# The S5 recurrence of a hybrid decoder step in chunks of four tokens

## The chip, the cores and the metric

The kernel runs as one program on one core of a Trainium2 chip. The metric is the device time of one execution in microseconds (us); the median of three runs of the kernel before is 1443.91 us (1443.73 to 1446.78).

## The reference, cut to what matters

One step of a single-layer decoder for a prompt of 512 tokens and 8 samples of one token each. Both are normalised, projected by `w_in`, sent through sparse attention (compressed, selected and window branches) and an S5 state-space branch, merged by gates, and sent through an MLP. The part that the change touches is the S5 branch: 32 groups of 16 channels, each with 64 complex states.

```python
def s5(u, h0, w):
    uc = u.reshape(b, t, S5_GROUPS, S5_CH)
    a_bar = exp(lam * dt)
    b_bar = ((a_bar - 1.0) / lam)[..., None] * b_c
    bu = einsum('gnc,btgc->btgn', b_bar, uc)
    h_t = a_bar * h_{t-1} + bu_t            # over the tokens, complex
    y = einsum('gcn,btgn->btgc', c_c, h).real + d * uc
    return y, h[:, -1]
...
z = gelu(y_s5)
o_s5 = z * sigmoid(z @ w['s5_w_glu'] + w['s5_b_glu'])
```

The last state of the prompt and the states of the samples are outputs too.

## The kernel before, in words

Everything is fp32. Activations lie transposed (`hT`: features on partitions, 520 columns: 512 prompt tokens and 8 samples). SyncE (queue SP) brings weights through three slabs of `stream`, in the order of `PLAN`; GpSimd (POOL) gathers the pages of the compression cache into the same slabs. A slab is filled when the slab three places ahead has been used (`slab_used`).

The projection stage, from about 22 to 280 us of the span, is a hand-written order of units for TensorE (PE): `HEAD_UNITS`, then `REST_UNITS`. A unit ("gemm", ...) is 16 matmuls of 128x128 weights on 260 columns (line 1710; each fp32 matmul is two records in the trace); "tr" transposes a K/V tile back to tokens on partitions (line 1687, five transposes). Units use two PSUM pairs in turn, so that unit u waits in `open_pair` until ScalarE (ACT) has evacuated unit u-2 (`pair_free`). ACT works the units off in the same order.

S5 is woven in. The 2048 complex states are 16 blocks of 128 states (2 groups each). The head transposes the padded B table in eight "bb" units, the rest begins with eight "cc" units for C, "h0" (sample states) and "bus" (their inputs, 32 small matmuls, line 1795). VectorE (DVE) builds tables of cos and sin of the state's angle, 512 tokens wide, for the first four blocks (`extend`, lines 1225 to 1230), POOL those of the later twelve. Then `s5_slot` is called 19 times behind the units of `SLOT_AFTER`: it computes B u of one block into PSUM (line 1803, 32 rows of weights, 512 columns) and the outputs of earlier blocks from their states (line 1821). Each block is one pass of the DVE loop (lines 1293 to 1316): rotate the inputs back by the angle, two real scans over 512 tokens, rotate forth. Such a pass waits for `bu_full` and releases `bu_free`, on which the next slot waits on PE; its end is `h_ready`, on which the output matmuls wait. The D term is added by DVE (`y_evac`, line 1256), the gelu is done on ACT after the stage (line 996).

When the stage ends, PE transposes the last states (`st_full`) and begins the compression stage: DVE transposes gathered rows (`permute`, line 1333), PE multiplies them with `w1c` (`layer1`, line 1864). Its first two halves come from the prompt's own rows with 128 columns, the later ones from the gathered slabs with 256. Key scores, selection, attention and the gated branches follow; from 742 us to the end PE works through the large products at line 2108.

## Time and profile before

| | |
|---|---|
| median of three runs | 1443.91 us (1443.73 to 1446.78) |
| span of the profiled execution | 1408.0 us |
| time of the profiled execution itself | not listed with the profile; the median lies 35.9 us above the span |
| PE busy, whole span | 1288.7 us, 92% |
| DVE busy | 935.1 us, 66% |
| ACT busy | 291.7 us, 21% |
| POOL busy | 423.6 us, 30% |
| mean granted TensorE clock | 0.974 |

### The profile page before, as it was taken

How to read it: one execution, taken by the hardware profiler on the slowest of the kernel's cores; microseconds unless marked ns; L12 is line 12 of the kernel's file. 1: busy time of each engine (PE TensorE's matmuls, PEld its weight loads, DVE VectorE, ACT ScalarE, POOL GpSimd, SP SyncE). 2: the span in 40 equal slices, each digit the busy share in tenths (PEclk: the TensorE clock that was granted, in tenths of full speed). 3: DMA queues.
4: the chain of work that ended last, by engine and by line, in shares of the span. 5: the costliest groups of instructions: out<-in, count | busy, mean ns of one | idle time of the engine just before them, and what ended most of it. 6: DMA issues, size and time to landing. Idle time of an engine off the chain costs nothing.

```text
span 1408.0 us, 19662 instructions
## 1 busy us (share of the span) xinstructions
PE 1288.7 (92%) x7155; PEld 1003.8 (71%) x7155; DVE 935.1 (66%) x1469; ACT 291.7 (21%) x849; POOL 423.6 (30%) x455
## 2 busy tenths in 40 slices
PE   5899899899988787889999999996999999999996
PEld 4677567577765554555577888785788888888885
DVE  7999999977763437776775565657565465466445
ACT  3311110010004455554421101014000000000012
POOL 5187290122255702222202111110111112423442
PEclk9999999999998999999999999997999999999998
DMA  8101461176664754433364313332112213122101
GB/s 272 61 16 35 94 133 60 60 264 253 257 215 145 240 180 117 136 117 103 126 240 136 105 60 105 133 123 75 58 62 71 109 60 119 61 73 107 60 1 61
DMA packets 122911, 165.59 MB, mean 118 GB/s; under 512 B 37504, under 2 KB 91312, under 8 KB 118464
## 3 DMA queue, kind: packets, MB, share of 16 engines
q1 hardware_dynamic: 105328, 104.69, 23.7%
q0 software_dynamic: 8080, 50.58, 10.1%
q10 hardware_dynamic: 9408, 9.07, 2.0%
q8 instruction: 57, 0.93, 0.3%
q14 instruction: 38, 0.31, 0.1%
HBM read 158.85 MB, written 13.84 MB: 123 GB/s over the span
## 4 chain that ended last, share of the span: by engine, by line
PE 69%; DVE 18%; issue 5%; ACT 4%; POOL 3%; DMA 1%; SPq 0%; DVEq 0%; PEldq 0%; ACTq 0%
PE PS L2108 42%; PE PS L1864 8%; PE PS L1710 6%; PE PS L1687 4%; POOL stream L801 3%; ACT R L1049 2%; DVE small L1499 2%; PE PS L1961 2%; PE PS L1993 2%; PE PS L2043 1%; DVE QO L1304 1%; DVE PS L1497 1%; DVE QO L1308 1%; DVE QO L1309 1%; DVE QO L1307 1%
## 5 line engine op out<-in xcount | busy, mean ns | idle before, releaser
L1710 PE MATMUL PS<-hT,stream 128*128 128x260 f32 (+1 forms) x800 | 182.2, 387 | 3.0 <-ACT small L957 1.0
L1710 PEld LDWEIGHTS PS<-hT,stream 128*128 128x128 f32 (+1 forms) x800 | 149.1, 189 | 36.3 <-issue 6.6
L2108 PE MATMUL PS<-R,stream 128*128 128x260 f32 x720 | 168.9, 383 | 2.4 <-PE PS L2108 2.4
L2108 PEld LDWEIGHTS PS<-R,stream 128*128 128x128 f32 x720 | 135.7, 190 | 25.8 <-issue 5.5
L2108 PE MATMUL PS<-R 128*128 128x260 f32 x576 | 130.8, 383 | 3.3 <-DVE R L1662 2.1
L1617 DVE TENSOR_TENSOR R<-PS,R 128x260 f32<-128x260 f32 x100 | 42.6, 426 | 126.1 <-PE PS L2108 125.0
L2108 PE MATMUL PS<-R,QO 128*128 128x260 f32 x544 | 123.6, 383 | 1.4 <-DVE QO L1543 1.4
L2108 PEld LDWEIGHTS PS<-R 128*128 128x128 f32 x576 | 109.3, 190 | 21.1 <-DVE R L1662 2.5
L1864 PE MATMUL PS<-R 128*128 128x256 f32 (+1 forms) x544 | 120.1, 377 | 2.7 <-PE PS L1864 2.3
L2108 PEld LDWEIGHTS PS<-R,QO 128*128 128x128 f32 x544 | 103.3, 190 | 17.6 <-DVE QO L1543 1.8
L1864 PEld LDWEIGHTS PS<-R 128*128 128x128 f32 x544 | 98.9, 190 | 20.9 <-issue 8.3
L1617 DVE TENSOR_TENSOR KVU<-PS,KVU 128x260 f32<-128x260 f32 x92 | 39.2, 427 | 101.2 <-PE PS L2108 90.8
L2108 PE MATMUL PS<-hT,stream 128*128 128x260 f32 x384 | 94.8, 390 | 3.7 <-PE PS L2108 3.1
L1687 PEld LDWEIGHTS PS<-consts,R 128*128 128x128 f32 (+2 forms) x465 | 49.6, 140 | 60.0 <-ACT R L1058 42.6
L1687 PE MATMUL PS<-consts,R 128*128 128x128 f32 (+2 forms) x465 | 65.9, 282 | 27.0 <-ACT R L1058 22.8
L580 POOL TENSOR_SCALAR R<-R,small 128x128 f32<-128x128 f32 (+3 forms) x64 | 48.4, 760 | 136.3 <-DVE small L1504 136.3
L2108 PEld LDWEIGHTS PS<-hT,stream 128*128 128x128 f32 x384 | 73.1, 193 | 18.7 <-issue 6.9
L1049 ACT ACTIVATE R<-PS,small 128x128 f32<-128x128 f32 (+3 forms) x128 | 66.1, 525 | 85.6 <-DVE small L1499 66.8
L1102 ACT ACTIVATE R<-PS 128x260 f32<-128x260 f32 x56 | 21.5, 386 | 270.4 <-PE PS L2108 270.4
L794 POOL DMA_INDIRECT stream<-in_cache_kv_cmp,row_cmp x32 | 31.7, 991 | 146.1 <-PEq L1853 82.2
L1333 DVE STREAM_TRANSPOSE R<-stream 128x2048 f32<-128x2048 f32 (+1 forms) x34 | 74.5, 2225 | 0.3
L801 POOL DMA_INDIRECT stream<-in_cache_kv_slc,row_kv x64 | 62.4, 976 | 40.5 <-issue 18.9
(373 smaller groups left out, 2107.9 us busy)
## 6 DMA issues: line engine op xcount, KB each, us to landing
stream<-in_cache_kv_slc SPq DMA_DIRECT2D x192, 128.0 KB, 2.2
stream<-in_w_mlp_up SPq DMA_DIRECT2D x8, 2048.0 KB, 8.7
stream<-in_w_mlp_down SPq DMA_DIRECT2D x8, 2048.0 KB, 8.6
stream<-in_w_in SPq DMA_DIRECT2D x4, 2048.0 KB, 11.7
stream<-in_state_kv_win SPq DMA_DIRECT2D x16, 512.0 KB, 7.5
stream<-in_w_in SPq DMA_DIRECT2D x8, 1024.0 KB, 18.8
out_kv_win_sample<-in_state_kv_win POOLq DMA_DIRECT2D x1, 8176.0 KB, 42.8
stream<-in_w_in SPq DMA_DIRECT2D x16, 256.0 KB, 4.5
```

Of the source, the lines that this page charges most:

```text
L580: return eng.tensor_scalar(S, S, ainv[:, k:k + 1], gtm[:, t, col:col + 1], ALU.mult, ALU.mult)
L794: pool.indirect_dma_start(slab(n)[:, 2048 * c:2048 * c + 2048], None, cmp_rows, bass.IndirectOffsetOnAxis(ap=row_cmp[:, 4 * b + 2 * half + ...
L801: pool.indirect_dma_start(dst[:, x, :], None, slc_rows, bass.IndirectOffsetOnAxis(ap=row_kv[:, at:at + 1], axis=0)).then_inc(rows_in[n % N ...
L1049: ins = nc.scalar.activation(PP[:, n % 2, j, c0:c0 + P * (t + 1)], score_block(n, j, c0), ACT.Exp, bias=amx[:, k:k + 1], accum_out=asm[:, ...
L1333: V.transpose(ROWST[:, w % 3, 0:256 * ns].rearrange("p (s x) -> p s x", x=256), slab(s)[:, 0:512 * ns].rearrange("p (s k x) -> p k s x", k ...
L1499: V.reduce_max(amx[:, k:k + 2 * nx], S[:, :, 0:P * (t + 1)], AX, negate=True).then_inc(as_max, 1)
L1617: V.tensor_tensor(to, product_of(w, i), other, ALU.add).then_inc(pr_added, 1)
L1687: return nc.tensor.transpose(out, in_, ident[0:rows, 0:rows])
L1710: ins = M(pair(u)[0:w, hf, 0:HALF], lhs[k], rhs[k][:, HALF * hf:HALF * hf + HALF], start=(k == 0), stop=(k == n - 1))
L1864: ins = M(out, w1c[:, kind, x, :], rhs, start=(x == 0), stop=(x == 7))
L1961: ins = M(score_block(n, j, c0), qT[64 * j:64 * j + 64, 4 * p + h + x, P * t:P * t + P], kT[64 * j:64 * j + 64, 2 * r + p, 0:P * (t + 1)], ...
L2108: ins = M(product_of(w, i), lhs[:, k, :], rhs[:, k, :], start=(k == 0), stop=(k == nk - 1))
```

## The change

The recurrence is taken in chunks of `TAU` = 4 tokens, so that only 128 chunk ends are scanned. For each block of states, the inputs of the four tokens of a chunk are stacked on 128 partitions (`UC`, 4 x 32 channels). ACT makes `UC` by 96 copies out of `uT` (`chunk_copies`, 24 behind each of four places). DVE builds a four-fold B table (`FP`, B times the powers 3 to 0 of the state factor); eight "ft" units transpose it to `ET`. `chunk_ends` multiplies `ET` with `UC`: the chunk sums of four blocks at once, 8 matmuls of 136 columns. DVE then does one pass for four blocks (512 columns: 4 blocks x 128 chunks, the two scans broken by zeros in the factor `DEC`), four passes in all. The tokens within a chunk come from the state at the chunk's start by a four-fold C table (`GP`, built by POOL from two "ct" units) and from the chunk's own inputs by a block-triangular table (`TO5`): its lags are the products `FP` x `C0P` of the "kk" unit (32 matmuls of 32 columns), with D added to lag 0, spread by ACT (`toeplitz`, 10 copies). A "y" unit gives the outputs of four blocks by 12 matmuls of 136 columns; ACT applies the gelu as it evacuates. The samples ride along as 8 of the 136 columns.

The cos and sin tables are now 128 wide and cover all 16 blocks; they lie in the memory of `FP`, so DVE widens them after "kk" is evacuated (`pair_free`, `U_KK + 1`). The first `chunk_ends` waits for `tables_done`. Gone are the units "bb", "cc", "bus", "ys", the 19 slots, POOL's tables, `y_evac`, and the gelu after the stage. SP's loads of the compression weights wait for `ends_full` 4 in place of `bu_full` 9.

```diff
-    head = u_tiles[:2] + [("bb", ri, q) for ri in range(2) for q in range(4)] + u_tiles[2:]
-    rest = [("cc", ri, q) for ri in range(2) for q in range(4)] + [("h0",), ("bus",)] + rest
+    head = u_tiles[:2] + [("ct", ri) for ri in range(2)] + u_tiles[2:3]
+    head += [("ft", ri, q) for ri in range(2) for q in range(4)] + u_tiles[3:]
+    rest.insert(1, ("h0",))
+    rest.insert(1, ("kk",))
+    for ii, behind in enumerate((("tr", 0, 3), ("tr", 1, 0), ("tr", 1, 2), ("tr", 1, 3))):
+        rest.insert(rest.index(behind) + 1, ("y", ii))
     rest.insert(len(rest) - 2, ("pos",))
...
+U_FT = UNITS.index(("ft", 0, 0))
+U_KK = UNITS.index(("kk",))
+U_Y = [UNITS.index(("y", ii)) for ii in range(4)]
+S_BEHIND = [UNITS.index(x) for x in (("kk",), ("tr", 0, 1), ("tr", 0, 2), ("tr", 1, 0))]
+COPIES_BEHIND = {("gemm", 0): 0, ("gemm", 1): 1, ("ft", 7): 2, ("gemm", 3): 3}
...
             wq = a["w_in"].rearrange("(k p) c -> p k c", p=P)
             slc = a["cache_kv_slc"].rearrange("n t k g d -> n t (k g d)")
             def compression_weights():
-                sp.wait_ge(bu_full, 9)
+                sp.wait_ge(ends_full, 4)
...
+            pool.wait_ge(pair_free, UNITS.index(("ct", 1)) + 1)
+            for k in range(TAU):
+                AR, AI = (x.unsqueeze(2).to_broadcast([P, NST, C5]) for x in apw[k])
+                nc.gpsimd.tensor_tensor(gwk[:, 0], CT5[:, 0], AR, ALU.mult)
+                nc.gpsimd.tensor_tensor(gwk[:, 1], CT5[:, 1], AI, ALU.mult)
+                nc.gpsimd.tensor_tensor(gwk[:, 2], CT5[:, 0], AI, ALU.mult)
+                link(nc.gpsimd.tensor_tensor(gwk[:, 3], CT5[:, 1], AR, ALU.mult))
+                for r, op in ((0, ALU.add), (1, ALU.subtract)):
+                    for g in range(2):
+                        rows, col = slice(64 * g, 64 * g + 64), 32 * k + 16 * g
+                        x, y = (0, 1) if r == 0 else (3, 2)
+                        ins = nc.gpsimd.tensor_tensor(GP[rows, r, :, col:col + C5], gwk[rows, x], gwk[rows, y], op)
+                link(ins)
+            pool.sem_inc(gp_ready, 1)
...
+            def chunk_copies(m):
+                act.wait_ge(pair_free, UNITS.index(("gemm", ("win", (C_U, 512)), m, P, ("u", m))) + 1)
+                act.wait_ge(zero_ready, 3)
                 for ii in range(4):
...
+                    rows = slice(32 * ii, 32 * ii + 32)
+                    for tau in range(TAU):
+                        nc.scalar.activation(UC[32 * tau:32 * tau + 32, 4 * m + ii, NB:NB + NK],
+                                             uT[rows, m, tau:T:TAU], ACT.Copy)
+                    nc.scalar.activation(UC[0:32, 4 * m + ii, 0:NB], uT[rows, m, T:NT], ACT.Copy)
+                    ins = nc.scalar.activation(UC[96:128, 4 * m + ii, NB + NK:UCW], uT[rows, m, T:NT], ACT.Copy)
+                ins.then_inc(chunks_ready, 1)
...
+            def toeplitz():
+                act.wait_ge(lag_ready, 1)
+                for lag in range(TAU):
+                    for row in range(TAU - lag):
+                        ins = nc.scalar.activation(
+                            TO5[32 * row:32 * row + 32, :, 32 * (row + lag):32 * (row + lag) + 32],
+                            KPS[32 * (TAU - 1 - lag):32 * (TAU - lag)], ACT.Copy)
+                ins.then_inc(toe_ready, 1)
...
+                    r = unit[1]
+                    if r == 0:
+                        act.wait_ge(zero_ready, 2)
+                    src = pr[:, 0, :].rearrange("p (i g c) -> p g i c", g=2, c=C5)
+                    for g in range(2):
+                        rows = slice(64 * g, 64 * g + 64)
+                        nc.scalar.activation(C0P[rows, r, :, 16 * g:16 * g + 16], src[rows, g], ACT.Copy,
+                                             scale=-1.0 if r else 1.0)
+                        ins = nc.scalar.activation(CT5[rows, r], src[rows, g], ACT.Copy, scale=-1.0 if r else 1.0)
+                elif kind == "kk":
+                    ins = nc.scalar.activation(KPS, pr[:, 0, :].rearrange("p (i c) -> p i c", i=NST), ACT.Copy)
...
+                elif kind == "y":
+                    ii = unit[1]
+                    rows = slice(32 * ii, 32 * ii + 32)
+                    src = pr[:, :, 0:2 * NCOL].rearrange("p h (m k) -> p h m k", m=2)
+                    for tau in range(TAU):
+                        nc.scalar.activation(uT[rows, :, tau:T:TAU].rearrange("p (h m) k -> p h m k", h=2),
+                                             src[32 * tau:32 * tau + 32, :, :, NB:NCOL], ACT.Gelu_apprx_tanh)
+                    ins = nc.scalar.activation(uT[rows, :, T:NT].rearrange("p (h m) b -> p h m b", h=2),
+                                               src[0:32, :, :, 0:NB], ACT.Gelu_apprx_tanh)
...
+                key = (kind, unit[2]) if kind == "gemm" and unit[4][0] == "u" else ("ft", u - U_FT) if kind == "ft" else None
+                if key in COPIES_BEHIND:
+                    chunk_copies(COPIES_BEHIND[key])
+                if unit == ("h0",):
+                    toeplitz()
...
+            for tau in range(TAU):
+                CR, CI = (x.unsqueeze(2).to_broadcast([P, NST, C5]) for x in bco[TAU - 1 - tau])
+                V.tensor_tensor(bwk[:, 0], bld[:, 0], CR, ALU.mult)
+                V.tensor_tensor(bwk[:, 1], bld[:, 1], CI, ALU.mult)
+                V.tensor_tensor(bwk[:, 2], bld[:, 0], CI, ALU.mult)
+                link(V.tensor_tensor(bwk[:, 3], bld[:, 1], CR, ALU.mult))
+                for r, op in ((0, ALU.subtract), (1, ALU.add)):
                     for g in range(2):
...
+                        rows, col = slice(64 * g, 64 * g + 64), 32 * tau + 16 * g
+                        ins = V.tensor_tensor(FP[rows, r, :, col:col + C5], bwk[rows, 2 * r], bwk[rows, 2 * r + 1], op)
+                link(ins)
+            dve.sem_inc(bb_ready, 1)
...
+            dve.wait_ge(pair_free, U_KK + 1)
+            V.tensor_copy(TAB[:, 0, :, 0:64], BAS[:, 0])
+            link(V.tensor_copy(TAB[:, 1, :, 0:64], BAS[:, 1]))
+            dve.wait_ge(power_ready, 8)
+            for half in range(2):
+                i8 = slice(8 * half, 8 * half + 8)
+                u_r, u_i = (x[:, i8].unsqueeze(2).to_broadcast([P, 8, 64]) for x in upw[7])
+                extend(TAB[:, 0, i8, 64:128], TAB[:, 1, i8, 64:128], TAB[:, 0, i8, 0:64], TAB[:, 1, i8, 0:64],
+                       u_r, u_i, (8, 64))
             dve.wait_ge(dve_ch, n_ch[0])
...
+            dve.sem_inc(tables_done, 1)
+            link(V.tensor_tensor(KPS[96:128], KPS[96:128], DI[96:128], ALU.add))
+            dve.sem_inc(lag_ready, 1)
...
+            for ii in range(4):
+                H = H5[ii % 2]
+                ct, st = (TAB[:, r, ii::4, :].rearrange("p (h m) t -> p h m t", h=2) for r in range(2))
+                hr, hi = (H[:, r, :, NB + 1:HW].rearrange("p (h m) t -> p h m t", h=2) for r in range(2))
+                V.tensor_copy(DEC.rearrange("p (m t) -> p m t", m=4),
+                              mag4[:, ii::4].unsqueeze(2).to_broadcast([P, 4, NK]))
+                if ii >= 2:
+                    dve.wait_ge(pair_full, U_Y[ii - 2] + 1)
+                V.memset(H[:, :, :, NB:NB + 1], 0.0)
+                for r in range(2):
...
+                br, bi = (PS[:, 4 + 2 * r:6 + 2 * r, 0:2 * NCOL].rearrange("p h (m k) -> p h m k", m=2)
+                          for r in range(2))
+                for r, b_ in enumerate((br, bi)):
+                    V.tensor_copy(buS[:, r, :, ii::4].rearrange("p b (h m) -> p h m b", h=2), b_[:, :, :, NK:NCOL])
+                b_r, b_i = br[:, :, :, 0:NK], bi[:, :, :, 0:NK]
+                V.tensor_tensor(t1, b_r, ct, ALU.mult)
+                link(V.tensor_tensor(t2, b_i, st, ALU.mult))
                 V.tensor_tensor(xr, t1, t2, ALU.add)
...
+                V.memset(DEC[:, 0:4 * NK:NK], 0.0)
+                link(V.tensor_tensor(xi, b_i, ct, ALU.mult))
+                V.tensor_tensor(t2, b_r, st, ALU.mult).then_inc(ends_free, 1)
+                dve.wait_ge(ends_free, ii + 1)
                 link(V.tensor_tensor(xi, xi, t2, ALU.subtract))
...
+                V.tensor_tensor_scan(f2, DEC, f2, 0.0, ALU.mult, ALU.add)
+                link(V.tensor_tensor_scan(f3, DEC, f3, 0.0, ALU.mult, ALU.add))
+                V.tensor_tensor(hr, ct, xr, ALU.mult)
...
                 dve.wait_ge(dve_ch, n_ch[0])
-                V.tensor_copy(hSp[:, 0, i:i + 1], hr[:, T - 1:T])
-                V.tensor_copy(hSp[:, 1, i:i + 1], hi[:, T - 1:T]).then_inc(h_ready, 1)
...
+                V.tensor_copy(hSp[:, :, ii::4], H[:, :, :, HW - 1]).then_inc(h_ready, 1)
+            sample_states()
...
+            dve.wait_ge(pair_full, U_Y[3] + 1)
...
+                elif kind == "kk":
+                    pe.wait_ge(pair_free, UNITS.index(("ct", 1)) + 1)
+                    for i in range(NST):
+                        for r in range(2):
+                            ins = M(pr[:, 0, 32 * i:32 * i + 32], FP[:, r, i, :], C0P[:, r, i, :],
+                                    start=(r == 0), stop=(r == 1))
+                elif kind == "y":
+                    ii = unit[1]
+                    pe.wait_ge(h_ready, ii + 1)
+                    if ii == 0:
+                        pe.wait_ge(gp_ready, 1)
+                        pe.wait_ge(toe_ready, 1)
+                    H = H5[ii % 2]
+                    for m in range(4):
+                        i = 4 * m + ii
+                        out = pr[:, m // 2, NCOL * (m % 2):NCOL * (m % 2) + NCOL]
+                        M(out, TO5[:, i, :], UC[:, i, 0:NCOL], start=True, stop=False)
+                        M(out, GP[:, 0, i, :], H[:, 0, m, 0:NCOL], start=False, stop=False)
+                        ins = M(out, GP[:, 1, i, :], H[:, 1, m, 0:NCOL], start=False, stop=True)
...
+            def chunk_ends(ii):
+                if ii == 0:
+                    pe.wait_ge(pair_free, U_FT + 8)
+                    pe.wait_ge(chunks_ready, 4)
+                    pe.wait_ge(tables_done, 1)
                 else:
...
+                    pe.wait_ge(ends_free, ii)
+                for r in range(2):
+                    for m in range(4):
+                        i = 4 * m + ii
+                        ins = M(PS[:, 4 + 2 * r + m // 2, NCOL * (m % 2):NCOL * (m % 2) + NCOL], ET[:, r, i, :],
+                                UC[:, i, NB:UCW], start=True, stop=True)
+                ins.then_inc(ends_full, 1)
...
+            for u, unit in enumerate(UNITS):
                 projection(u, unit)
-            pe.wait_ge(pair_free, UNITS.index(("bb", 1, 3)) + 1)
-            s5_slot(0)
```

## Rows read from the trace of the kernel before

**Rows 1.** Windows by stage: length, busy us (instructions), clock, DMA share, GB/s.

```profile
56.00:151.00 95.00, 91.50 (x536) 68.57 (x536) 92.56 (x109) 16.52 (x42) 67.22 (x54) 0.98 0.24 65
...
270.00:281.00 11.00, 7.24 (x24) 2.30 (x23) 10.24 (x19) 1.55 (x5) 3.19 (x3) 0.84 0.53 191
...
281.00:425.00 144.00, 137.57 (x630) 108.92 (x628) 105.14 (x93) 9.01 (x16) 47.04 (x51) 0.98 0.69 246
```

**Rows 2.** Waits of PE from 22 to 281 us: total, times, longest.

```profile
PE PS L1803 <- DVE QO L1297: 3.8, 2, 3.5
...
PE PS L1821 <- DVE small L1316: 3.6, 1, 3.6
```

**Rows 3.** Timeline of PE: start, length, line, operation, count, idle before.

```profile
36.18 0.60 PE L1687 MATMUL PS<-consts,R 128*128 128x128 f32 x4
...
41.56 14.29 PE L1710 MATMUL PS<-hT,stream 128*128 128x260 f32 x64
...
65.64 1.97 PE L1795 MATMUL PS<-KVU,R 32*128 32x8 f32 x64 [0.72 <-ACT small L948]
...
78.28 7.28 PE L1710 MATMUL PS<-hT,stream 128*128 128x260 f32 x32
...
93.47 1.13 PE L1803 MATMUL PS<-KVU,R 32*128 32x512 f32 x4
...
96.36 0.77 PE L1687 MATMUL PS<-consts,QO 128*128 128x128 f32 x5
...
154.73 2.08 PE L1803 MATMUL PS<-KVU,R 32*128 32x512 f32 x4 [3.52 <-DVE QO L1297]
...
160.29 7.28 PE L1710 MATMUL PS<-hT,stream 128*128 128x260 f32 x32
...
240.07 1.13 PE L1803 MATMUL PS<-KVU,R 32*128 32x512 f32 x4
...
242.11 7.28 PE L1710 MATMUL PS<-hT,stream 128*128 128x260 f32 x32
...
263.42 7.28 PE L1710 MATMUL PS<-hT,stream 128*128 128x260 f32 x32
...
279.85 0.66 PE L1687 MATMUL PS<-consts,small 128*128 128x128 f32 x4
...
280.34 11.03 PE L1864 MATMUL PS<-R 128*128 128x128 f32 x64
```

**Rows 4.** Windows of 2 us where PE works after a wait.

```profile
158.00:160.00 2.00, 2.00 (x4) 0.18 (x1) 1.93 (x4) 0.00 (x0) 0.00 (x0) 0.50 0.00 0
...
160.00:162.00 2.00, 2.00 (x9) 1.51 (x9) 1.93 (x4) 0.00 (x0) 0.00 (x0) 0.94 0.00 0
```

**Rows 5.** Chain of waits, a full-clock run of 128-column matmul records: start, us.

```profile
280.51 3.59 PE PS L1864 x32
```

**Rows 6.** Timeline of PE, 62-column matmuls with full weights.

```profile
476.06 1.90 PE L1947 MATMUL PS<-R,QO 128*128 128x62 f32 x16
```

**Rows 7.** Timeline of ACT: first and last of four 128-column copies in a row.

```profile
280.54 0.29 ACT L965 ACTIVATE QO<-PS 128x128 f32<-128x128 f32 x1 [7.48 <-PE PS L1687]
...
281.03 0.27 ACT L966 ACTIVATE QO<-PS 16x128 f32<-16x128 f32 x1
```

**Rows 8.** Timeline of DVE: start of two table extensions, one recurrence pass.

```profile
49.03 0.70 DVE L1225 TENSOR_TENSOR PS<-R,small 128x512 f32<-128x512 f32 x1
...
52.89 0.70 DVE L1225 TENSOR_TENSOR PS<-R,small 128x512 f32<-128x512 f32 x1
...
265.45 0.68 DVE L1293 TENSOR_TENSOR QO<-PS,R 128x512 f32<-128x512 f32 x1
...
276.16 0.14 DVE L1316 COPY small<-QO 128x1 f32<-128x1 f32 x1
```

**Rows 9.** Timeline of POOL: the gather into the last freed slab.

```profile
271.06 1.58 POOL L794 DMA_INDIRECT stream<-in_cache_kv_cmp,row_cmp  x1 [36.59 <-PEq L1750]
```

**Rows 10.** Window of 2 us while that gather runs.

```profile
274.00:276.00 2.00, 0.00 (x0) 0.00 (x0) 1.96 (x3) 0.00 (x0) 0.03 (x1) 1.00 0.86 352
```

343 lines of the change are left out of this document (113 added, 230 removed).

## Prediction

> **What bounds the kernel now.** I read the windows by stage first. From 56 to 151 us PE is busy 91.5 of 95 us and DVE 92.6: in the projection stage both are full. The last 11 us of it are different: PE 7.2 busy, DVE 10.2, clock 0.84. In the compression stage behind it PE is busy 137.6 of 144 us [rows 1]. Then the waits of PE within the stage: DVE makes PE wait 3.5 us once in front of a slot's input products (line 1803) and 3.6 us once in front of the last outputs (line 1821); the rest is small [rows 2]. So PE's own work sets the time of the stage, and DVE's sixteen recurrence passes, spread over the whole of it, touch the end at two places. The timeline of PE shows what these cost: after the first wait it works from 154.73 to 160.29 on a slot's worth of products, after the second from 276.36 to about 280.3 [rows 3], with the granted clock at 0.5 and back at full speed just after 160 [rows 4]; 0.5 is the 1.2 GHz level. The reader is to see that a S5 product costs PE time even where DVE is on time, and that each DVE wait is paid about one and a half times.
>
> Everything after the stage starts from PE's reaching line 1864 at 280.34 [rows 3] (call it T). I take the later stages as shifted whole, so the forecast is the new T. 0.2% of this kernel is 2.9 us, about what a measurement can tell from no change.
>
> **The stage up to the second K/V product, 78.28 us before.** PE ends the second U product at 36.18 as before. The two "ct" units are each like one "bb" unit (4 transposes; eight take 41.56 - 36.18 = 5.4 us [rows 3]): 1.3 us, to 37.5. The third U product waits in `open_pair` for the evacuation of ct 0, and in ACT's queue the 24 copies behind the second U product come first. That product's evacuation ends near 37.0. A copy of 128 columns takes (281.03 - 280.54)/3 = 0.163 us start to start [rows 7]: sixteen are 2.6 us. The eight of 8 columns cost less than that each; I take 0.1, 0.8 us. Then four copies of 256 columns for ct 0, twice 0.163 each, 1.3 us: 41.7. So PE waits 4.2 us, which is new, and by the two cases above I add a clock loss: half of 5.6 us and half of 3.9 us are 2.8 and 2.0 [rows 3 to 5]; I take 2.4. From 41.7: third U product 7.1, eight "ft" units 5.4, fourth U product 7.1, first K/V product 7.1, clock 2.4: 70.8. DVE's four-fold table is 32 operations of 256 columns; even at the 0.64 us of a 512-column one (six in 52.89 - 49.03 = 3.86 us [rows 8]) it is ready before "ft" starts at 48.8. It hides, as does POOL's `GP` (wanted by the first "y" only).
>
> "kk" is 32 matmuls, 64 records of full 128x128 weights with 32 columns. No such shape ran before. From above: 62-column matmuls with full weights take 1.90/16 = 0.119 us a record [rows 6], and 32 records of 128 columns 3.59/32 = 0.112 [rows 5]; equal times for 62 and 128 columns say that the weights set the pace. From below: columns alone, a quarter of 0.112, would be 1.8 us in all. I take 0.112: 7.2 us, to 78.0. Were it at half clock, 14.3.
>
> Now the wait that I hold to be the change's price. DVE may widen the tables only when ACT has evacuated "kk" (0.8 us with latency, 78.8), and the first `chunk_ends` stands right behind "kk" in PE's order and waits for `tables_done`; everything later on PE, beginning with "h0" and the second K/V product, queues behind it. DVE: two copies of 1024 columns (at most two 0.64 each, at least half that; 1.3 together), two extensions 7.7 us [rows 8]: 87.8. PE idle 9.8 us. Then `chunk_ends` (16 records of 136 columns, 0.112 x 136/128 = 0.119: 1.9 us), "h0" 0.5, clock loss 2.4: the second K/V product starts at 92.6, 14.3 us later than before, although "cc", "bus" and two slots are gone.
>
> **From there to T.** Removed on PE: three slots with a third product, 96.36 - 93.47 = 2.9 us each, nine shorter ones of 242.11 - 240.07 = 2.04, the one with the first DVE wait 3.5 + 5.6 = 9.1, the last ones from 270.5 (263.42 and a product of 7.1) to 279.85, 9.3 [rows 3], and "ys", 64 tiny records for which I take 0.9 us; the like of them in "bus" took 1.97 [rows 3]. Sum 8.7 + 18.4 + 9.1 + 9.3 + 0.9 = 46.4. Added: three `chunk_ends` of 1.9, four "y" of 24 records x 0.119 = 2.9, sum 17.3, and 0.8 at the end, where the last evacuation has no slot to hide behind. T = 280.3 + 14.3 - 46.4 + 18.1 = 266.3, so 14.0 us earlier.
>
> DVE's loop starts once "h0" is evacuated, near 93. A pass took 276.3 - 265.45 = 10.8 us [rows 8]; the new one has the same twelve large operations and two scans on 512 columns, and some 1.3 us of small ones: 12. Passes 1 and 2 end near 105 and 117. The third waits for the first "y" (127 to 130) and ends at 142, the fourth for the second "y" and ends at 155; their outputs are wanted near 159 and 170. So DVE leaves the path. Cover gone: a pass would have to take 25 us. ACT's `toeplitz` (10 copies of 512 columns, four times 0.163 each, 6.5 us) ends by 101, wanted at 127; its gelus lie beside K/V products. SP's load of the compression weights waits for the fourth `chunk_ends` at 140, before it waits for the q slab (about 158); the next q slab is then issued some 10 us later than before and wanted 36 us later. It hides.
>
> **A rule against it.** PE ran 128-column records with full weights 0.112 us apart [rows 5], so a load hides behind the records before it. The Trainium skill, TensorE: Matmul & The Clock Gate, section The mechanism, says that a weight load overlaps matmuls in flight only when the row group differs. The old input products sat in four row groups; every new S5 matmul uses all rows, and by that rule each load would stand in the open. The rows say no: at 0.112 a record nothing is added to the columns' time. I keep it as a rival.
>
> **Sum.** 1443.9 - 14.0 = 1429.9 us (span 1408.0 before, 1394 after; the 35.9 us between span and median stay).
>
> **Rivals.**
> - *Loads in the open* (slower). If the 160 records of `chunk_ends` and "y" and the 64 of "kk" paid 0.112 for the load and then their columns, that is 160 x 0.112 + 1.8 = +19.7 us, so 1449.6. It decides the sign from 0.062 us a record on. Against it stand rows 5; for it only that the shapes are new.
> - *ACT holds the head.* If a copy of every fourth token costs three times the 0.163, 24 copies are 10 us in place of 3.4: the first 24 delay the second U product's evacuation by some 3 us and the second 24 hold PE 7 us more: 1440. No row shows a copy from such a strided source, for or against.
> - *The table wait is longer, or "kk" runs slow.* "kk" at 1.2 GHz adds 7.2, so 1437. The clock fell before only behind a wait of 3.5 us and more [rows 3, 4], which speaks against it, but a unit of 7 us with 32 columns a record did not occur.
> - *Given back behind T.* The last gathered slab was issued at 271.06, 9.3 us before T [rows 9], and used 11.9 after it. Now it is issued 1 us before T. 2 MB at 352 GB/s [rows 10] are 6 us, transposing 2.2; at the 246 GB/s of the stage [rows 1] 8.5. The slack is 2 us, or none: up to +3, so 1433.
> - *The waits cost less.* No clock loss and quicker tables and "kk": -8, so 1422.
>
> **How the numbers follow.** The forecast with its range 1424 to 1436 gets 0.60; the waits cost less, below 1424, 0.08; longer waits (slow "kk", ACT, gather together) 1436 to 1441, 0.14; their sum eats the gain, within 2.9 us, 0.07; slower 0.11, of it 0.05 for loads in the open and 0.06 for ACT and "kk" at once being worse than bounded. So faster 0.82, same 0.07, slower 0.11. The bounds of the unknown terms, "kk" -5 to +7, copies +7, clock -5 to +1, table copies +1.3, gather +3, give 1421 to 1441 when no two big ones meet.
>
> **What would show it.** PE idle 4 us in front of the third U product and 10 us behind "kk", each followed by windows at 0.5; the second K/V product near 92.6; "kk" 7 us long, a "y" 2.9; four DVE passes of 12 us, none waited for; line 1864 first at 266. Wrong would be: records of 136 columns well over 0.12 us, ACT copies well over 0.17, or a wait of PE for the gathered slab 12 us behind T.

## The result and the profile after

The changed kernel takes 1448.84 us (median of 20 runs, 1444.06 to 1455.89), the kernel before 1445.12 beside it on the same chip (20 runs, 1441.87 to 1450.69): ratio 1.0024, 95% interval 1.0014 to 1.0035. Forecast were 1429.9 us and a gain. On five other chips the kernel before has medians of 1410.7 to 1413.4 us, about 35 us less; on the one of them where both were timed many times they stand level: 1410.57 us (12 runs) against 1410.72 (29 runs), ratio 0.9998, interval 0.9985 to 1.0011. A seventh chip is slow like the first (1435.24 us, one run of the kernel before). So the change wins nothing, and the question is where 14 us went.

The profiled run took 1447.94 us for a span of 1446.2: launch and end are 1.7 us, not 35.9 us. The span of 1408.0 us in the kernel before's profile fits none of its 20 runs on this chip (the fastest took 1441.87) but those on the faster chips, so I had read the 35.9 us out of a span and a median that do not belong together. T, the first matmul of the compression stage (line 1864 before, line 1887 now), lies at 283.1 in it; in a second trace of the kernel before, taken in the first experiment, it lies at 283.1 too, against 280.3 in the one the prediction was made from. The timeline of TensorE (PE) after, as [rows 3]:

```profile
28.14 17.29 PE L1753 MATMUL PS<-hT,stream 128*128 128x260 f32 x64 [0.74 <-DVE hT L1180]
48.59 1.12 PE L1730 MATMUL PS<-consts,R 128*128 128x128 f32 x4 [2.72 <-ACT KVU L931]
58.68 8.67 PE L1753 MATMUL PS<-hT,stream 128*128 128x260 f32 x32 [8.98 <-ACT KVU L972]
...
87.25 9.13 PE L1814 MATMUL PS<-R 128*128 128x32 f32 x64
106.35 3.55 PE L1853 MATMUL PS<-QO,R 128*128 128x136 f32 x16 [9.97 <-DVEq L1296]
...
109.96 7.18 PE L1753 MATMUL PS<-hT,stream 128*128 128x260 f32 x32
...
283.11 1.17 PE L1887 MATMUL PS<-R 128*128 128x128 f32 x9
```

Everything behind 109.96 is as forecast: from there to T 173.2 us, forecast 173.7. All 16.8 us by which T misses its 266.3 arise before. The first product starts at 28.14 and not at 22.05; the second unit of C transposes and the third U product wait 2.72 and 8.98 us for ACT. The same stretch in the timelines of DVE and POOL shows the late start:

```profile
4.19 1.84 POOL L731 DMA_DIRECT2D R<-in_s_b_re  x2
5.79 8.39 DVE L1201 COPY QO<-QO 16x128 f32<-16x128 f32 x1 [4.92 <-DMA QO<-in_s_log_dt]
...
7.63 0.99 POOL L734 MEMSET R<- 128x1024 f32 x1
8.51 3.56 POOL L735 MEMSET R<- 128x4096 f32 x1
11.97 1.85 POOL L736 MEMSET R<- 128x2048 f32 x1
...
13.86 0.25 POOL L738 MEMSET QO<- 128x128 f32 x1
```

DVE's first copy, 16x128 elements, lasts 8.39 us and ends at 14.18, with POOL's last fill (a fill is a memset to zero). PE, ACT and the norms hang on it. Before, POOL had its second fill there (4.19 to 7.70) and the copy took 2.28 us, to 7.77; the changed kernel fills `C0P`, `GP`, `TO5` and `UC` instead, behind the loads of B. ACT's groups from 0 to 110 us, by form (busy, mean ns of one):

```profile
L891 ACT ACTIVATE QO<-KVU 32x128 f32<-32x128 f32 x64 | 27.4, 429 | 0.8
```

A copy of every fourth token takes 0.429 us, start to start 0.44, where I had 0.163 from [rows 7]; the 24 of a block (the eight of 8 columns start 0.22 apart) take 8.8 us, not 3.4. Windows of the four long PE entries above (length, busy, clock last but two):

```profile
28.14:45.43 17.29, 17.29 (x66) 14.51 (x67) 16.17 (x64) 6.76 (x18) 13.50 (x47) 0.82 0.33 104
58.68:67.35 8.67, 8.67 (x34) 7.28 (x35) 0.33 (x1) 1.27 (x4) 6.91 (x11) 0.84 0.00 0
87.25:96.38 9.13, 9.12 (x65) 8.99 (x63) 0.00 (x0) 4.82 (x14) 0.00 (x0) 0.77 0.01 4
106.35:109.90 3.55, 3.55 (x18) 3.55 (x19) 1.87 (x6) 0.00 (x0) 0.00 (x0) 0.58 0.02 5
```

Length times clock gives each entry's length at full speed: 14.2, 7.3, 7.0 and 2.06 us. So the products are the same as before, "kk" is near the 7.2 us of the forecast, and the rest, 3.1, 1.4, 2.1 and 1.5 us, is what the level of 1.2 GHz cost. Three of the four stand behind idle time of PE, as in [rows 4]; for the first one the idle time alone does not explain it, since in the run spread below the same idle time stands ahead of it and it takes 14.29 us, full speed. "kk" does not: PE was busy without a gap before it and all through it, and the clock fell inside it.

```profile
85.00:87.20 2.20, 2.20 (x11) 1.91 (x11) 0.00 (x0) 2.13 (x7) 0.00 (x0) 1.00 0.95 369
...
89.00:91.00 2.00, 2.00 (x21) 2.00 (x20) 0.00 (x0) 1.93 (x7) 0.00 (x0) 1.00 0.00 0
91.00:93.00 2.00, 2.00 (x18) 2.00 (x17) 0.00 (x0) 1.19 (x4) 0.00 (x0) 0.82 0.00 0
93.00:95.00 2.00, 2.00 (x11) 2.00 (x11) 0.00 (x0) 0.00 (x0) 0.00 (x0) 0.50 0.00 0
```

### The profile page after: what moved, and what is told of

The parts are those of the page before. It is cut to its first block, busy times and chain, and to the rows that moved or that the text cites. A ratio compares the mean times of both kernels' runs of the same rounds, so it can differ in the third digit from the quotient of the medians.

```text
span 1446.2 us, 19447 instructions
## 1 busy us (share of the span) xinstructions
PE 1288.8 (89%) x7099; PEld 1030.6 (71%) x7099; DVE 783.6 (54%) x1320; ACT 347.4 (24%) x964; POOL 349.6 (24%) x422
## 4 chain that ended last, share of the span: by engine, by line
PE 78%; DVE 9%; ACT 6%; issue 4%; another core or an unknown queue 2%; DMA 0%; DVEq 0%; POOL 0%; ACTq 0%; PEldq 0%
PE PS L2130 41%; PE PS L1753 13%; PE PS L1887 7%; PE PS L1730 6%; ACT R L1079 2%; DVE small L1542 2%; PE PS L1984 2%; PE PS L2016 2%; PE PS L1944 1%; PE PS L2066 1%; ACT QO L891 1%; DVE PS L1540 1%; DVE R L1376 1%; ACT R L1088 1%
## 5 line engine op out<-in xcount | busy, mean ns | idle before, releaser
L1887 PE MATMUL PS<-R 128*128 128x256 f32 (+1 forms) x544 | 125.2, 386 | 11.5 <-issue 5.8
L2130 PEld LDWEIGHTS PS<-R 128*128 128x128 f32 x576 | 109.3, 190 | 21.1 <-DVE R L1705 2.5
L1730 PEld LDWEIGHTS PS<-consts,stream 128*128 128x128 f32 x320 | 41.7, 164 | 54.4 <-issue 31.4
```

Source lines behind the costliest of these rows:

```text
L1730: return nc.tensor.transpose(out, in_, ident[0:rows, 0:rows])
L1887: ins = M(out, w1c[:, kind, x, :], rhs, start=(x == 0), stop=(x == 7))
L2130: ins = M(product_of(w, i), lhs[:, k, :], rhs[:, k, :], start=(k == 0), stop=(k == nk - 1))
```

## The experiments

Times are medians; each run's ratio is to the kernel before on its own chip. First both kernels once more, after that single edits, then several at once.

**before_again** 

> The kernel before, unchanged, profiled once more. In the profile of the changed kernel the stage up to the first record of the compression stage is 3.3 us shorter than in the profile of before (counted from the first U product), but what follows it is 35.4 us longer (1163.1 against 1127.7 us), with idle of TensorE put down to issue; yet 20 runs of each differ by 0.24% only. Theory 1: the profiled execution of before (span 1408.0) was not a typical one, and the like of those 35 us is in an ordinary execution of before too: span 1440 to 1446, with TensorE idle by issue behind the stage. Theory 2: before has none of it and its span is near 1408 again; then the change brings the 35 us and the 35.9 us between span and median of before are launch.

**after_again** 

> The changed kernel, unchanged, profiled once more beside it. Theory 1: first U product to first compression record 255 us again within 1 (it is set by TensorE's own order and three waits), and what follows it within 1163 plus or minus 5. Theory 2: the 35 us behind it come and go from run to run, so it can be anywhere from 1128 to 1163.

Measured 1411.33 us (span 1409.5) and 1410.08 (span 1408.3). The stages of both from the first record at their lines: the stage behind T lasts 148.7 and 148.5 us, from T to the end 1126.4 and 1125.1. So nothing is given back behind T, and the changed kernel does not bring the 35 us: they are absent from both traces here (neither theory had the 1125 us of the second) and belong to the chip. In all sixteen traces on the faster chips, of every version, T to the end takes 1125.1 to 1129.6 us. In the trace of the 1447.94 us run 1163.1 us lie behind T, most of the difference in two stretches. The windows, first of that run, then of after_again, over about the same code:

```profile
414.00:428.00 14.00, 6.20 (x17) 3.81 (x18) 3.47 (x4) 0.00 (x0) 5.37 (x7) 0.71 0.37 112
460.00:530.00 70.00, 47.57 (x270) 27.76 (x271) 17.73 (x36) 23.78 (x42) 35.63 (x37) 0.78 0.50 156
```

```profile
412.00:426.00 14.00, 10.20 (x43) 7.05 (x42) 6.34 (x8) 0.63 (x1) 10.58 (x12) 0.91 0.74 219
460.00:530.00 70.00, 57.08 (x445) 37.38 (x448) 28.02 (x63) 39.46 (x77) 27.18 (x31) 0.98 0.68 216
```

The DMA engines move 112 and 156 GB/s on the one chip, 219 and 216 on the other; the code there is untouched by the change. Whether the slower transfers are the cause or go with it, and what on that chip does this, wasn't tried.

**after_timed** 

> The changed kernel as it is, timed beside the kernel before on one chip, so that the runs below can be set against it there. Theory 1 (the two stand as in the twenty runs): ratio 1.000 to 1.004. Theory 2 (the 2.4 per thousand belong to the chip of those runs): ratio 0.996 to 0.999, as the single run of 1410.08 us against 1411.33 us has it. The waits of TensorE as in the two traces of this kernel so far: 14.3 us for the copy at L1201, 9.0 for the evacuation at L972, 10.0 for the tables.

Measured 1410.57 us, the ratio of 0.9998 given above; waits 14.3, 9.4 and 10.0 us. It lies between the two theories: level. T in the three traces of this kernel: 283.1, 283.2, 282.9.

**dense_copies**: each copy takes 128 tokens in a row and leaves out the step of four tokens.

```diff
-                                             uT[rows, m, tau:T:TAU], ACT.Copy)
+                                             uT[rows, m, NK*tau:NK*tau+NK], ACT.Copy)
```

> The changed kernel with the 64 copies of the chunk inputs reading 128 consecutive tokens of uT in place of every fourth one (so the S5 branch gets the wrong tokens; everything else is computed). Theory stride: a copy takes 0.43 us because its source steps over 16 bytes; dense it starts every 0.17 us, 24 of them take some 4 us in place of 8.9, TensorE's waits of 2.7 and 9.0 us in front of the third U product shrink to 0 and about 4, and the time falls by 8 to 11 us against the changed kernel. Rival, partitions: a copy costs 0.43 us because it moves between partitions 32 at a time; then nothing changes. Rival, given back: the waits shrink but what is won is lost behind the stage; then the time falls by less than 3 us.

Measured 1406.83 us, ratio 0.9955 (0.994 to 0.9971), T 281.1. ACT's copies:

```profile
L891 ACT ACTIVATE QO<-KVU 32x128 f32<-32x128 f32 x64 | 19.7, 307 | 0.8
```

The stride costs 0.12 us of the 0.43; a copy without it still costs 0.31, almost twice my price. The wait before the third U product falls from 9.0 to 7.5 us, the one before the second C transposes from 2.7 to 0.7. So the stride is a real part but not the whole; the rival "nothing changes" is out.

**copy_sources**: the sixteen copies of the first block from four kinds of source, so that this block is left without its own tokens. 

> What a copy of 32 partitions by 128 columns costs ScalarE by the kind of its source, measured in the sixteen copies of the first U block: four from uT (SBUF) with 128 columns in a row, four from PSUM in a row, four from uT with every second column, four from PSUM with every second column. They replace the copies of every fourth column there, so the S5 branch gets wrong tokens for this block; those of the other blocks stay. My price came from copies out of PSUM in a row, 0.163 us start to start. Theory 1 (both the source's memory and the stride count): PSUM in a row near 0.17 to 0.25, SBUF in a row 0.31 as in the run with dense copies, SBUF with a stride between that and 0.43. Theory 2 (the 32 partitions or their shift count, not the memory): PSUM in a row costs 0.3 as well. The Trainium skill, VectorE: DVE Perf Modes, section on the TRN2 errata, gives ScalarE 224 cycles plus the columns from SBUF and 172 from PSUM at 1.2 GHz; by that page alone the two would be 0.293 and 0.250 us.

Measured 1439.51 us in one run, the kernel before beside it 1435.24, on the second slow chip (1157.4 us from T to the end). The timeline of ACT, in fours: SBUF in a row, PSUM in a row, SBUF every second column, PSUM every second:

```profile
37.76 1.27 ACT L993 ACTIVATE QO<-KVU 32x128 f32<-32x128 f32 x4
39.05 1.11 ACT L995 ACTIVATE QO<-PS 32x128 f32<-32x128 f32 x4
40.17 1.31 ACT L997 ACTIVATE QO<-KVU 32x128 f32<-32x128 f32 x4
41.49 1.12 ACT L1000 ACTIVATE QO<-PS 32x128 f32<-32x128 f32 x4
```

Start to start 0.32, 0.28, 0.33 and 0.28 us: the source's memory makes 0.04, a step of two columns 0.01, a step of four 0.12. Theory 1 fails (PSUM in a row costs 0.28, not 0.17 to 0.25); theory 2 comes near, and the memory is the small part. My row of 0.163 was of copies that overlap. What lets them is visible in the changed kernel's own trace, in ACT's copies of the C table, 256 columns each:

```profile
57.32 0.38 ACT L970 ACTIVATE R<-PS 64x256 f32<-64x256 f32 x1
57.60 0.36 ACT L972 ACTIVATE KVU<-PS 64x256 f32<-64x256 f32 x1
57.98 0.38 ACT L970 ACTIVATE R<-PS 64x256 f32<-64x256 f32 x1
```

The first two use the same partitions and start 0.28 us apart; the third goes to the other 64 partitions and starts 0.38 us later, when the one before it has ended. The same pattern, 0.28 and 0.37 to 0.40, stands in the traces of after_timed, vector_copies and spread_start. The copies of [rows 7] all begin at partition 0; every chunk copy, and every copy of this run, writes to other partitions than the one before it. So of the 0.28 us between 0.163 and 0.44 about 0.12 go with the lost overlap, 0.04 with the memory and 0.12 with the step of four. The first part is read from traces; no edit isolated it. The Trainium skill, VectorE: DVE Perf Modes, section on the TRN2 errata, has cycle counts from which 0.293 and 0.250 us follow as an estimate: the order and the difference of 0.04 agree, both measured ones are 0.03 higher. The Trainium skill, SBUF — State Buffer, section Door 1: The DMA port swizzle, says that accesses that leave a line of 16 bytes pay; that is a step of four fp32, and steps of two and four stand on the two sides of it here.

**vector_copies**: DVE makes the copies of the first three blocks behind its tables.

```diff
-COPIES_BEHIND = {("gemm", 0): 0, ("gemm", 1): 1, ("ft", 7): 2, ("gemm", 3): 3}
+COPIES_BEHIND = {("gemm", 3): 3}
...
+            for m in range(3):
+                chunk_copies(m)
             dve.wait_ge(pair_free, U_KK + 1)
```

> One edit: the chunk copies of the first three U blocks are made by VectorE behind its tables of powers (it is idle from 59 to 97 us) and no longer by ScalarE; those of the fourth stay. Theory 1 (ScalarE's 0.44 us a copy, 8.8 us a block, holds its evacuations, and these hold TensorE): the waits of 9.0 us before the third U product and of 2.7 us before the second C transposes go, and the third U product takes 7.2 to 8.7 us; the second compression stage starts at 269 to 272 instead of 283.1. Theory 2 (TensorE waits here for something else as well, or runs at half clock as long): under 5 us are won. VectorE's copy of 32x128 with a stride is not in any trace so far; I expect 0.2 us, and 0.45 us would still fit into its idle time.

Measured 1402.77 us, ratio 0.9938 (0.9926 to 0.995). Both waits for ACT are gone, but T is 276.5, not 270:

```profile
46.03 7.28 PE L1767 MATMUL PS<-hT,stream 128*128 128x260 f32 x32 [0.54 <-ACT KVU L972]
...
73.20 10.44 PE L1828 MATMUL PS<-R 128*128 128x32 f32 x64
98.52 3.97 PE L1867 MATMUL PS<-QO,R 128*128 128x136 f32 x16 [14.88 <-DVEq L1310]
```

The third U product starts 11.3 us earlier than in after_timed (57.38). It runs at full clock, so "kk" starts 13.9 us earlier; 2.4 us of this go back in "kk" (10.44 for 8.06, clock 0.67 for 0.88) and 4.9 in the wait for the tables (14.9 for 10.0): DVE's copies aren't done when "kk" is. The first two fours took 3.02 and 2.87 us while POOL built `GP`, the later ones 1.10. The profiled run was the slowest of six, 3.3 us above the median, so a typical T lies lower. The Trainium skill, SBUF — State Buffer, section Who interferes with whom, says that DVE's copies in a two-port mode and POOL block each other whole; 0.75 against 0.28 us a copy goes with it.

**kk_early**: "kk" ahead of the fourth U product. 

> The changed kernel with the unit kk moved in front of the fourth U product (copies of the third block behind it), and the first chunk sums behind h0: DVE widens the tables beneath the fourth U and the first K/V product. Theory: the wait of 10.0 us on tables_done and the clock loss behind it go, less what kk's wait for its evacuation costs: the time falls by 8 to 12 us against the changed kernel. Rival, given back: the first compression record comes 8 to 12 us earlier and the time falls by less than 3 us, since the gathers and the instruction fetch behind it set the end. Rival, ACT: the copies behind kk and behind the fourth U product (9 us each) hold TensorE instead: a fall of 3 to 7 us with a new wait in front of the first chunk sums.

```diff
-    head += [("ft", ri, q) for ri in range(2) for q in range(4)] + u_tiles[3:]
+    head += [("ft", ri, q) for ri in range(2) for q in range(4)] + [("kk",)] + u_tiles[3:]
```

The third block's copies stand behind it, the first chunk ends behind "h0".

Measured 1406.12 us, ratio 0.9951 (0.9935 to 0.9967), T 277.0. The table wait of 10.0 us is gone, one of 2.0 for the last copies in its place; T comes 6 us earlier than in after_again, and the time is 4.0 us under that single run: the rival "ACT", 3 to 7 us. "kk" takes 10.08 us here and the product behind it 9.50.

**late_memsets**: `GP` and `TO5` are filled behind the powers, near 50 us (`toeplitz` then waits for `gp_ready` too). 

> One edit: GpSimd fills GP and TO5 with zeros (3.56 and 1.85 us) behind its products of powers, near 50 us, where it idles, instead of at the start. Theory 1 (VectorE's copy at L1201 takes 8.39 us because these fills run beside it, and TensorE, left idle, does the first two U products at half clock): the copy takes about 2.3 us, the first U product starts near 22.5 us instead of 28.1, the two take 14.3 us instead of 17.3, and the third U product starts 9 to 10 us earlier, since ScalarE's row of copies hangs on the end of the first product; the first record of the second compression stage falls from 283.1 to 273 to 275, the time by as much. Theory 2 (the copy is long for another reason, its own form or its input): it stays at 8.4 us and nothing moves. Theory 3 (the fill beside VectorE's table work near 50 us costs there what it saved): the chunk ends start no earlier.

**late_memsets_again** 

> The kernel of late_memsets once more, for the moment at which its copy of log_dt arrives. There it started at 5.60 us and took 0.47; in six runs with the fills at the start it started at 5.63 to 6.33 and took 7.9 to 8.6. Theory A (the fills hold it): 0.3 to 0.6 us again wherever it starts ahead of the first late load at 6.0 us, and to 8.9 us, the end of the short fills, if it starts behind. Theory B (a matter of the moment, before or after 5.6 us): if it starts at 5.65 or later it is held to 8.9 us, whatever else.

**loads_behind_fills**: the loads of B are issued behind all fills. 

> One half of the start alone: GpSimd issues the loads of B behind its fills; the copy of log_dt stays with VectorE. The fills then follow each other without a break from 0.74 to 10.7 us, and the copy arrives at 5.5 to 6.3 us within the fill of GP (5.08 to 8.59). Theory A (VectorE gets through when the fill that runs ends, as its operations at 7.3 and 8.65 us did in the run of the start alone): the copy ends near 8.7 us, the first U product starts at 23 to 24 us. Theory B (it gets through only when GpSimd has nothing more in its queue): it ends at 10.7 us, the first U product starts at 25 to 26. Theory C (the loads of B held it in the changed kernel, not the fills): it takes 0.3 us.

**start_only**: the same, and the copy of L1201 is made by ACT. 

> The start alone: the copy of log_dt (L1201) is made by ScalarE, and GpSimd issues the loads of B behind its fills. GP and TO5 are filled at the start as in the changed kernel. Theory 1 (VectorE's copy is held by the fills, and the gains land later since the loads of B are issued 3.5 us sooner than in the kernel before): the first U product starts at 22 to 23.5 us instead of 28.1, without anything moved to 50 us. How much of these 5 to 6 us reaches the end depends on TensorE's clock: with the late fills 3.8 us earlier became 0.3 us in the profiled run, because the products behind ran at half clock for longer; I expect the time 2 to 5 us under the changed kernel, ratio to the kernel before 0.996 to 0.999. Theory 2 (the copy is long whatever the engine): no change.

```diff
-            V.tensor_copy(nat[:, 2, :].rearrange("p (g n) -> p g n", g=2),
-                          ldt2.unsqueeze(2).to_broadcast([NST, 2, N5])).then_inc(nat_ready, 1)
...
+            nc.scalar.activation(nat[:, 2, :].rearrange("p (g n) -> p g n", g=2),
+                                 ldt2.unsqueeze(2).to_broadcast([NST, 2, N5]), ACT.Copy).then_inc(nat_ready, 1)
```

| | first U product | T | time, ratio |
|---|---|---|---|
| after_timed | 28.2 | 282.9 | 1410.57, 0.9998 |
| late_memsets | 24.4 | 282.6 | 1408.43, 0.9977 (0.9965 to 0.999) |
| late_memsets_again | 24.4 | 279.2 | 1407.26, one run |
| loads_behind_fills | 22.9 | 277.4 | 1406.10, 0.9962 (0.9948 to 0.9977) |
| start_only | 21.6 | 276.2 | 1405.43, 0.9958 (0.9945 to 0.9972) |

With the long fills away the copy takes 0.47 us (from 5.60) and 0.29 (from 6.05), so the moment doesn't decide. What is odd is that POOL's timeline is the same in these runs and in the changed kernel up to 8.5 us: when the copy starts POOL is issuing loads, the fills that were taken away would come 2.5 us later, and yet with them it lasts 7.9 to 8.6 us (five traces). In loads_behind_fills it is let through when a fill ends, theory A:

```profile
5.08 3.51 POOL L730 MEMSET R<- 128x4096 f32 x1
5.57 3.10 DVE L1201 COPY QO<-QO 16x128 f32<-16x128 f32 x1 [4.70 <-DMA QO<-in_s_log_dt]
8.53 1.88 POOL L731 MEMSET R<- 128x2048 f32 x1
```

In start_only ACT makes this copy in 0.31 us beside the same fills, and two small operations of DVE with one input are held in its place, each to the end of one fill; one with two inputs (L1207, 7.09) takes 0.17 us beside the same fill:

```profile
7.29 1.32 DVE L1209 TENSOR_SCALAR small<-small 128x16 f32<-128x16 f32 x1
8.53 1.83 POOL L731 MEMSET R<- 128x2048 f32 x1
8.65 1.74 DVE L1210 TENSOR_SCALAR small<-small 128x16 f32<-128x16 f32 x1
```

Of the 14.3 us that PE waited, the late fills take away 8, but the first product comes only 3.8 us earlier: DVE then waits until 14.3 for the norm's gains (`norm_mix_pre`, `norm_mlp_pre`), whose loads take 9.7 us from issue to landing there. In start_only, with the loads of B behind the fills, they take 6.4 and 6.8 us and the gains are there at 11.5. So the early loads of B, ahead of the long fills, are a second cost beneath the first: alone they leave the first product at 24.4, against 22.05 in the trace of before, which had them behind its second fill (gains 7.1 and 7.4 us). Then the clock: the two first products took 17.27 us at 0.82 in late_memsets, "kk" 10.70 at 0.65, and a start 3.8 us earlier became 0.3 at T; with the same kernel in its second run (15.98 us, and "kk" 8.10) it became 3.7. What an edit at the head brings is blurred by some 3 us in one trace. The profiled run of late_memsets was also the slowest of its 12, 5.8 us above the median; by the medians the late fills bring 2.1 us.

**all_three**: late fills, "kk" early, all copies on DVE behind the tables. 

> Three edits at once: the fills late, all chunk copies on VectorE, and the products for the lags ahead of the fourth U product, so that the tables are ready when the chunk ends are due. If the three costs lie one behind the other on TensorE, their sum goes: 6 for the start, 3 for its clock, 12 for the copies, 6 for the tables as measured, 27 us in all, the second compression stage at 254 to 258 and the time 24 to 28 us under the changed kernel's beside it, ratio 0.980 to 0.984 to the kernel before. If what is won at the head is given back further on (the window loads and gathers that the earlier stage starts sooner), the stages behind it get longer by it and the time falls by less than 15.

Measured 1410.29 us, ratio 0.9992 (0.9981 to 1.0002), T 281.2: nothing. The timeline of PE says why:

```profile
53.21 9.99 PE L1829 MATMUL PS<-R 128*128 128x32 f32 x64
...
103.70 3.97 PE L1868 MATMUL PS<-QO,R 128*128 128x136 f32 x16 [23.29 <-issue]
```

The waits between the first products are gone, and one of 23.3 us stands behind them. DVE's tables took from 63.9 to 77.2 (13.3 us with POOL's products beside them, 9.0 in vector_copies), its 96 copies from 78.5 to 103; the first chunk ends need both. The costs did not lie one behind the other on PE; moved to one engine they made a new chain of 40 us.

**spread**: "kk" early, copies divided. **spread_start**: the same, and start_only.

```diff
+COPIES_BEHIND = {("ft", 7): 0, ("kk", 0): 1, ("gemm", 3): 2}
...
             dve.sem_inc(lag_ready, 1)
+            chunk_copies(3)
```

> The products for the lags early, as in the run with kk early, and the chunk copies spread: ScalarE makes those of the first block behind the eighth transposition of C, of the second behind the lags' evacuation, of the third behind the fourth U product's; VectorE those of the fourth behind its tables. Nothing is held on the chain of the head, and VectorE is free for the tables, which it wasn't in the run with all three edits (its copies stood behind the tables there, and TensorE waited 23.3 us for them). Theory 1 (the costs of the head add up when no copy stands on the chain): third U product at 46, lags 58.6 to 68.5, tables done at 78.5, the first chunk ends at 86 to 88, the second K/V product at 89 to 91 instead of 109.3, the second compression stage at 262 to 266, ratio to the kernel before 0.985 to 0.989. Theory 2 (TensorE's clock or VectorE beside GpSimd takes half of it): second compression stage at 270 or later, ratio above 0.990.

> Both together, the spread copies and the start. If the start's gain adds to the spread one: second compression stage 3 to 6 us earlier than with the spread copies alone, ratio 0.981 to 0.987. If it goes into half clock again: within 1 us of the spread copies alone.

Measured 1393.20 us, ratio 0.9867 (0.9852 to 0.9882), T 264.5, and 1386.64 us, ratio 0.9818 (0.9804 to 0.9831), T 258.5. Theory 1 in spread, and the start adds its whole 6 us. The first products run at full clock (14.29 us) in both traces, but that is not what it takes: in spread_start_again below they took 17.16 us, and T still came at 259.0, because "kk" (9.34 us for 10.00), the product behind it (8.58 for 9.58) and the wait before the chunk ends (3.2 for 3.9) were shorter. spread_start's timeline:

```profile
22.03 14.29 PE L1766 MATMUL PS<-hT,stream 128*128 128x260 f32 x64 [0.73 <-DVE hT L1182]
...
50.71 10.00 PE L1827 MATMUL PS<-R 128*128 128x32 f32 x64
60.52 9.58 PE L1766 MATMUL PS<-hT,stream 128*128 128x260 f32 x32
...
81.75 3.46 PE L1866 MATMUL PS<-QO,R 128*128 128x136 f32 x16 [3.87 <-issue]
85.00 5.34 PE L1766 MATMUL PS<-hT,stream 128*128 128x260 f32 x22
```

The second K/V product starts at 85.0, against 109.3 in after_timed; behind T nothing is lost (148.2 us for the next stage). This version beats the kernel before, side by side on one chip, by 25 us; the changed kernel wasn't timed on that chip. "kk" and the U product behind it still take 5 us more here than at full clock.

**lags_split**: spread_start with "kk" in halves, one ahead of the "ft" units and one behind. **spread_start_again** as its measure.

```diff
+    head += [("kk", 0)] + [("ft", ri, q) for ri in range(2) for q in range(4)] + [("kk", 1)] + u_tiles[3:]
```

> The kernel of spread_start with its kk unit in two halves: the first 32 records ahead of the transpositions to ET, the last 32 behind them. In every trace kk began at full clock with PE busy before it and fell to 0.5 some 4 to 4.5 us after its start, while PE stayed busy; the 64 records took 10.00 us there and the U product behind them 9.58. Theory 1 (an unbroken run of records with 32 columns brings the clock down): each half takes 3.5 to 3.7 us at 1.0, the U product 7.2 to 7.3; 5 us less on PE. How much arrives is bounded by DVE's and ACT's work up to the first chunk ends, which PE waited 3.9 us for: the tables start 2.5 us earlier, so the second K/V product starts 2 to 3 us earlier, T at 255.5 to 257, ratio 0.979 to 0.981. Theory 2 (the clock falls there for another reason, a budget of the whole head): the sum of the two halves stays at 9 us or more, or the next product takes over 9.

> The kernel of spread_start once more beside lags_split, on the same chip, as its measure: ratio 0.980 to 0.983, kk at 10.0 to 10.6 us, T at 258 to 259.

Measured 1390.62 us, ratio 0.984 (0.9822 to 0.9859), T 261.3, beside 1387.61, ratio 0.9824 (0.9806 to 0.9842), T 259.0: split is no better, rather 3 us worse (the intervals overlap). The timeline of lags_split, and windows from its first half on:

```profile
44.90 4.18 PE L1829 MATMUL PS<-R 128*128 128x32 f32 x32
48.89 6.90 PE L1744 MATMUL PS<-consts,R 128*128 128x128 f32 x32
55.79 4.98 PE L1829 MATMUL PS<-R 128*128 128x32 f32 x32
60.59 9.39 PE L1767 MATMUL PS<-hT,stream 128*128 128x260 f32 x32
```

```profile
45.00:47.00 2.00, 2.00 (x21) 2.00 (x19) 1.93 (x6) 0.60 (x1) 1.86 (x4) 1.00 0.00 0
47.00:49.00 2.00, 2.00 (x15) 2.00 (x15) 1.97 (x6) 0.00 (x0) 1.88 (x3) 0.71 0.00 0
...
56.00:58.00 2.00, 2.00 (x20) 2.00 (x19) 1.97 (x3) 1.97 (x5) 1.92 (x3) 1.00 0.05 12
58.00:60.00 2.00, 2.00 (x12) 2.00 (x11) 1.29 (x2) 1.93 (x7) 1.92 (x4) 0.52 0.00 0
```

The halves sum to 9.16 us and the product behind takes 9.39, which is what theory 2 put down; but the windows side with the first theory's cause. The clock falls within either half, and now the transpositions between them pay too, 6.90 us for 5.4: splitting made one fall into two. My "in every trace some 4 to 4.5 us after its start" was wrong: in late_memsets the window from 2 to 4 us behind "kk"'s start is already at 0.86, in after_timed it is at 1.00 up to 6 us behind it. Wider records for these products weren't tried.

## Why the prediction was wrong

What the change removes behind the head was right, the head was mis-sized. T came at 283.1 and not 266.3; the 16.8 us by the terms of my sum, in the trace of the 1447.94 us run:

- **"PE ends the second U product at 36.18 as before": failed**, +9.1. The change moves POOL's fills and loads at the start, and I didn't follow POOL there, though the diff changes it. The fills hold DVE's first copy, and the first product starts 6.1 us later; the gains, delayed by the early loads of B, lie hidden beneath and alone cost 2.3 us of it (late_memsets). PE then does the first two products at 0.82: 3.1 us, and this part is luck. With the same start they took 17.34, 15.98 and 14.29 us (after_again, after_timed, spread), with an early start 14.29 and 17.16 (spread_start and its second run), and 15.98 in before_again. Shown by loads_behind_fills, start_only and the two runs with late fills. What holds the copy for all of 8.39 us, through the ends of several fills, stays open: where the fills ran without the loads between them it got through at the end of the one that ran.
- **The third U product at 41.7: failed**, +7.9. The step is the copy at 0.163 us; measured 0.44, a block 8.8 for 3.4. The row was of copies from PSUM, in a row and all from partition 0; the new ones lack all three. From the end of the second U product to the third 13.4 us passed, forecast 5.5, with a second wait in it (2.7 us, the first block's copies ahead of an evacuation), which my sum put at nothing. The rival "ACT holds the head" had it at the right size (copies of 10 us) and had it only within the 0.14 of longer waits and, together with "kk", the 0.06. Shown by vector_copies, where both waits are gone.
- **From there to the second K/V product**: forecast 50.9 us, measured 51.3. The table wait was 10.0 for 9.8. "kk" was right at full clock, 7.0; its 2.1 us above it come from the clock, as 1.4 and 1.5 at the two other places. I had 4.8 us for the clock in this stretch and it took 5.0: right in sum by luck, wrong in cause, since I took [rows 3, 4] to say that the clock falls only behind a wait of 3.5 us and more. In "kk" it fell while PE was busy. The trace of before had a warning that I left out, a product at clock 0.83 behind waits of 0.72 and 1.01 us and the 64 records of 8 columns of [rows 3]:

```profile
68.61 8.68 PE L1710 MATMUL PS<-hT,stream 128*128 128x260 f32 x32 [1.01 <-ACT small L957]
```

- **From there to T**: forecast 173.7, measured 173.2. Chunk ends 2.02 us for 1.9. The first "y" unit ran from 144.98 to 147.87, 2.9 us as forecast, 0.12 us a record. DVE was waited for nowhere. The terms differ from trace to trace more than their sum: in after_timed the first products took 15.98 us, the third 9.81 and "kk" 8.06, and T is 282.9.
- **Loads in the open**: refuted by those 0.12 us; the Trainium skill's rule on row groups, in TensorE: Matmul & The Clock Gate, section The mechanism, would by my pricing have made it 0.22 and does not show here; the same section also lets a load run ahead into a background buffer for the weights, which would fit.
- **Given back behind T**: refuted, 148.5 us against 148.7 for the stage.
- **"The 35.9 us between span and median stay"**: wrong reading without effect on the difference. It is 1.7 us for launch and end, the rest the chip.
- **"The bounds of the unknown terms give 1421 to 1441"** do not follow from the terms: -5 and -5 give 1420, +7, +1, +1.3 and +3 (without the copies' +7) 1442. It changed nothing.

The chance of 0.07 for no change was too small since the copies were priced from one row, and the late start, 6.1 us of the 16.8, was no term at all. That the ratio is 1.0024 on one chip and 0.9998 on others is not explained: on the former only the changed kernel was profiled.

## What to carry to other kernels

When a change adds or drops a fill, a load or a memset on one engine's queue, follow that queue from time zero: a fill on GpSimd costs nothing until VectorE has a copy beside it. TensorE can pay for a wait a second time in clock: the product behind the waits of 7.5 to 9.5 us took 8.67 to 10.34 us, 7.28 without the wait. A row of back-to-back operations gives the price of its own case only; for many small copies look for a row with the same source, stride and change of partitions, and bound the price from above by the duration of one, not by the best spacing of four. And where several waits stand on a chain, removing each gains its part, but moving all their work to one idle engine can gain nothing; the gain came when each piece went to the engine that was idle at that moment.
